# Taking the first 32 key tiles of the U table whole: turned and multiplied for all tokens on TensorE, gelu in pairs

## What is computed

```python
ia = jnp.take_along_axis(top_i[:, :, 0], best_c // K, axis=-1)
ib = jnp.take_along_axis(top_i[:, :, 1], best_c % K, axis=-1)
expert = ia * PEER_N_KEYS + ib
gate = jax.nn.softmax(best_s, axis=-1)
...
a = jnp.einsum('td,ted->te', xb, u_tab[eb])
hidden = gb.astype(xb.dtype) * jax.nn.gelu(a)
return jnp.einsum('te,ted->td', hidden, v_tab[eb])
```

## Time and profile before

| | us |
|---|---|
| median of three runs | 3085.14 |
| lowest, highest | 3076.94, 3086.59 |
| the profiled execution, its span | 3083.2 |
| first U row starts, last ends on VectorE | 1829.4, 2736.5 |
| busy in the span: TensorE, VectorE, ScalarE, POOL | 2723.6, 2111.9, 1146.2, 988.0 |

### The profile page before, as it was taken

One profiled execution on the slowest core, in us unless ns is written; L12 is line 12 of the kernel. 1 busy time (PEld: TensorE's weight loads), 2 busy tenths in 40 slices (PEclk: granted clock), 3 DMA queues, 4 the chain that ended last, 5 costly groups with the idle time before them and its releaser, 6 DMA issues.

```text
span 3083.2 us, 34652 instructions
## 1 busy us (share of the span) xinstructions
PE 2723.6 (88%) x12212; PEld 1969.0 (64%) x12212; DVE 2111.9 (68%) x2870; ACT 1146.2 (37%) x1980; POOL 988.0 (32%) x567
## 2 busy tenths in 40 slices
PE   9999999999999999999999975666666877669997
PEld 8888788888887888999889872222223433235433
DVE  5687665555564545445566688887888887679877
ACT  5455555555553335445665530000002330034000
POOL 0021000000000000000000038777778777878864
PEclk9999999999999999999999997898999888988999
DMA  7444455555555555453354459999999999999997
GB/s 271 151 155 164 173 178 183 189 190 190 190 177 191 184 185 183 178 182 135 127 191 173 164 228 415 419 409 410 408 417 411 416 407 402 420 376 383 409 402 305
DMA packets 123586, 827.89 MB, mean 269 GB/s; under 512 B 22167, under 2 KB 22183, under 8 KB 23855
## 3 DMA queue, kind: packets, MB, share of 16 engines
q0 software_dynamic: 79392, 510.36, 40.8%
q1 hardware_dynamic: 43920, 313.73, 28.5%
q10 hardware_dynamic: 144, 2.10, 0.2%
...
## 4 chain that ended last, share of the span: by engine, by line
PE 58%; POOL 14%; DMA 11%; DVE 9%; issue 5%; ACT 3%; DVEq 0%; SPq 0%; ACTq 0%
PE ps L608 49%; POOL rows L1324 14%; DMA rows<-peer_u,arena 7%; PE ps L1230 2%; DMA rows<-peer_v,arena 2%; DMA rows<-peer_v 2%; DVE arena L2449 2%; PE ps L1241 2%; DVE WL L506 1%; PE ps L716 1%; ACT arena L1800 1%; DVE arena L209 1%; DVE arena L202 1%; PE ps L916 0%; DVE arena L203 0%
## 5 line engine op out<-in xcount | busy, mean ns | idle before, releaser
L506 DVE SCALAR_TENSOR_TENSOR WL<-ring,PA,WH 128x512 fp32r<-128x512 f32 x896 | 633.1, 753 | 461.7 <-ACT WH L490 445.1
L1241 PE MATMUL ps<-rows,rstd 128*128 128x512 f32 x1164 | 629.6, 694 | 300.1 <-DMA rows<-peer_v,arena 216.9
L2449 DVE CUSTOM_DVE_ANT_0 arena<-rows,arena 128x2048 f32<-128x2048 f32 x256 | 586.9, 2293 | 155.7 <-DMA rows<-peer_u,arena 128.9
L1241 PEld LDWEIGHTS ps<-rows,rstd 128*128 128x128 f32 x1164 | 245.8, 221 | 670.5 <-issue 371.9
L1324 POOL DMA_INDIRECT rows<-peer_v,arena x256 | 484.0, 1891 | 196.8 <-DVE arena L2449 73.4
L489 ACT ACTIVATE WH<-ring,PA 128x512 fp32r<-128x512 f32 x448 | 324.2, 724 | 550.1 <-PE ps L608 401.7
L1324 POOL DMA_INDIRECT rows<-peer_u,arena x256 | 451.4, 1763 | 165.7 <-DVE WL L506 85.9
L608 PE MATMUL ps<-WH,HH 128*128 128x512 f32 x1120 | 442.8, 395 | 4.0 <-DVE WL L506 4.0
L608 PE MATMUL ps<-WH,HL 128*128 128x512 f32 x1120 | 438.0, 391 | 0.0
L608 PE MATMUL ps<-WL,HH 128*128 128x512 f32 x1120 | 437.9, 391 | 0.0
L490 ACT ACTIVATE WH<-ring,PA 128x512 fp32r<-128x512 f32 x448 | 317.2, 708 | 0.0
...
## 6 DMA issues: line engine op xcount, KB each, us to landing
ring<-stream SPq DMA_DIRECT2D x292, 1024.0 KB, 4.8
rows<-peer_v POOLq DMA_DIRECT2D x32, 1024.0 KB, 15.4
rows<-peer_u,arena POOLq DMA_INDIRECT x256, 14.8
rows<-peer_v,arena POOLq DMA_INDIRECT x256, 15.0
...
```

The source lines that it names most:

```text
L506: ins = nc.vector.scalar_tensor_tensor(out=half_tile(WL, u)[:, s], in0=raw_half(u)[:, s], scalar=gain[d], in1=half_tile(WH, u).bitcast(f32 ...
L1241: last = mm(ps[:, 4 * tt + q, :], DIAG[:, k % DIAGS, :], rows[:, SLOTS[n % ROWS], q * CH:(q + 1) * CH], start=n == mine[0], stop=n == ends[q])
L2449: ins = V.tensor_tensor_reduce(out=JUNK, in0=rows[:, SLOTS[n % ROWS], :], in1=HN[:, tt, :], scale=1.0, scalar=0.0, op0=ALU.mult, op1=ALU.a ...
```

## The change

- The 32 first tiles of U are loaded whole, too (`"turned"` entries, 2 per group in groups 0 to 7, 4 in groups 8 to 11, none later). TensorE transposes each, 16 blocks of 128 x 128 (`turn_u`, four parts of four), ScalarE copies each part to SBUF (`keep_turned_u`), and TensorE multiplies it with the transposed activations `HNT` for all 256 tokens (`u_products`, 16 products of 128 x 128 by 128 x 256). The parts 0 and 1 are transposed at the tile's entry; the rest (`finish_u`) comes after the next V row of TensorE, or before the next tile.
- Two tiles share a PSUM bank, and gelu is done for the pair, 128 x 512 elements: square and tanh on ScalarE (`square_u`, `tanh_u`), `poly_u` and `gelu_u` on VectorE, at fixed distances in `ROW_ORDER` (2, 5, 8 and 11 entries after the tile is finished).
- The batches now give gates instead of gate times gelu (`turn_ids` turns `GB`); VectorE multiplies them into the stored gelu (`weigh_dense`, two operations per batch), instead of ScalarE's copy. All 16 batches come in groups 12 to 15, one every 3.5 U rows.
- U gathers use the ids that leave the first 32 tiles out (one list, `IDU`; two copies fewer per `choose`).
- `choose` comes every 12 U rows from the 11th on, the last in group 9; `weigh` (three small operations) is split from `finish`.
- 9 V rows in groups 1 to 7 and 12 to 15, 5 in groups 8 to 11: 119 instead of 135 in the U stage (407 entries with the tiles) and 137 in the last. There one in eight V rows goes to TensorE (18 in all, 9 before), 119 to VectorE (112 before), and the V tiles start after V row 10 instead of 35.
- Before the first entry TensorE transposes `HN` (32 blocks) and ScalarE copies the result.

```diff
-LEAD = 9
 BATCH = 16
 BATCHES = P // BATCH
-DENSE_FROM, TAIL, SHARED = 35, 8, 3
-RING_OF = (16, 32)
+DENSE_FROM, TAIL, SHARED = 10, 8, 3
+LEADS = [0] + [9] * 7 + [5] * 4 + [9] * 4
+U_TILES = [2] * 8 + [4] * 4 + [0] * 4
+U_AFTER = {0: (), 2: (5, 12), 4: (1, 5, 9, 13)}
+PART_AT = (0, 6144, 12288, 10240)
+U_PARTS = (0, 2, 1, 3)
+U_ORDER = [8 * part + i for part in U_PARTS for i in range(8)]
 V_ORDER = [(g, j) for g in range(GROUPS) for j in range(PEER_K)]
-N_LEAD = LEAD * (GROUPS - 1)
...
     if m < 0:
         return True
-    if m < DENSE_FROM:
-        return m % 5 == 4
+    if m < N_LAST - TAIL:
+        return m % 8 == FIRST_V1 % 8
     return m in (N_LAST - TAIL + 1, N_LAST - TAIL + 3)
 ROW_ORDER = []
-_v = 0
+_v = _d = 0
 for _g in range(GROUPS):
     for _j in range(PEER_K):
         ROW_ORDER.append(("u", _g, _j))
-        if _g and LEAD * _j // PEER_K != LEAD * (_j + 1) // PEER_K:
+        if LEADS[_g] * _j // PEER_K != LEADS[_g] * (_j + 1) // PEER_K:
             ROW_ORDER.append(("v", *V_ORDER[_v]))
             _v += 1
-assert _v == N_LEAD
+        if _j in U_AFTER[U_TILES[_g]]:
+            ROW_ORDER.append(("turned", _d, 0))
+            _d += 1
+assert _v == N_LEAD and _d == N_DENSE
 ROW_LAST = len(ROW_ORDER)
 _d = 0
...
-_count = {"dve": 0, "pe": 0}
+RAW_TURNED = 24
+_count = {"dve": 0, "pe": 0, "turned": RAW_TURNED}
 for _tab, _g, _j in ROW_ORDER:
-    _by = "pe" if _tab == "dense" or _tab == "v" and by_matmul(PEER_K * _g + _j - N_LEAD) else "dve"
-    _count[_by] += 1
+    _by = "turned" if _tab == "turned" else "pe" if _tab == "dense" or _tab == "v" and by_matmul(PEER_K * _g + _j - N_LEAD) else "dve"
+    _count[_by] += 4 if _by == "turned" else 1
     ROW_DONE.append((_by, _count[_by]))
+FINISHED_AT = {}
+for _n, (_tab, _g, _j) in enumerate(ROW_ORDER):
+    if _tab == "turned":
+        FINISHED_AT[_g] = next(n for n in range(_n + 1, ROW_LAST) if ROW_ORDER[n][0] in ("v", "turned"))
+SQUARE_AT, POLY_AT, TANH_AT, GELU_AT = ({FINISHED_AT[2 * p + 1] + later: p for p in range(N_DENSE // 2)} for later in (2, 5, 8, 11))
 BATCH_AT = {}
-for _b in range(BATCHES):
-    BATCH_AT[ROW_AT["u", 9 + _b // 2, 3 + 8 * (_b % 2)]] = (0, _b)
-    BATCH_AT[ROW_AT["v", *V_ORDER[N_LEAD + 4 * _b + 3]]] = (1, _b)
-TURN_AT = {ROW_AT["u", 8, 3]: 0, ROW_LAST: 1}
+for _n in range(TT * BATCHES):
+    _g, _j = divmod(12 * PEER_K + 8 + 7 * _n // 2, PEER_K)
+    BATCH_AT[ROW_AT["u", _g, _j]] = divmod(_n, BATCHES)
+TURN_AT = {ROW_AT["u", 12, 4]: 0, ROW_AT["u", 14, 0]: 1}
 KEEP_AT = {n + 3: b for n, b in BATCH_AT.items()}
 ONE_HOT_AT = {n - 3: b for n, b in BATCH_AT.items()}
+U_ROWS = [(g, j) for g in range(GROUPS) for j in range(PEER_K)]
+CHOOSE_AT, GATE_AT, WEIGH_AT = ({ROW_AT["u", *U_ROWS[10 + 12 * (g - EARLY) + later]]: g for g in range(EARLY, GROUPS)} for later in (0, 3, 6))
+WEIGH_AT.update({ROW_AT["u", 0, 3 + 2 * g]: g for g in range(EARLY)})
 LAST_DENSE = ROW_AT["dense", N_DENSE - 1, 0]
 N_ROWS = len(ROW_ORDER)
...
+            def turn_u(n, d, part):
+
+                q = 4 * d + part
+                if part == 0:
+                    pe.wait_ge(sem(f"row_in{n % ROWS}"), 16 * (n // ROWS + 1))
+                if q >= 2:
+                    pe.wait_ge(sem("transposes_kept"), TT + q - 1)
+                else:
+                    pe.wait_ge(sem("norm_leading"), 8 * len(TURNED) + 8)
+                for k in range(4):
+                    at = (4 * part + k) * P
+                    last = nc.tensor.transpose(ps[:, 6 + q % 2, k * P:(k + 1) * P], rows[:, SLOTS[n % ROWS], at:at + P], ident)
+                last.then_inc(sem("raw_turned"), 1)
+
+            def u_products(d, part):
+
+                q = 4 * d + part
+                if d % 2 == 0 and part == 0 and d >= 4:
+                    pe.wait_ge(sem("gelu_done"), 1 + d // 2 - 1)
+                pe.wait_ge(sem("transposes_kept"), TT + q + 1)
+                for k in range(4):
+                    kt = 4 * part + k
+                    last = mm(ps[:, 4 + d // 2 % 2, d % 2 * TOK:(d % 2 + 1) * TOK], UT[q % 2][:, k, :], HNT[kt // 8][:, kt % 8, :],
+                              start=kt == 0, stop=kt == KD - 1)
+                last.then_inc(used, 1)
+
+            def finish_u(n, d):
+
+                u_products(d, 0)
+                turn_u(n, d, 2)
+                u_products(d, 1)
+                turn_u(n, d, 3)
+                u_products(d, 2)
...
-                    pool.wait_ge(sem(f"rows_{by}"), count)
-                if tab == "dense":
-                    pool.dma_start(rows[:, SLOTS[n % ROWS], :], v_tab[g * PEER_KEYS:(g + 1) * PEER_KEYS, :]).then_inc(sem(f"row_in{n % ROWS}"), 16)
+                    pool.wait_ge(sem({"dve": "rows_dve", "pe": "rows_pe", "turned": "raw_turned"}[by]), count)
+                if tab in ("dense", "turned"):
+                    table, ia = (v_tab, g) if tab == "dense" else (u_tab, U_ORDER[g])
+                    pool.dma_start(rows[:, SLOTS[n % ROWS], :], table[ia * PEER_KEYS:(ia + 1) * PEER_KEYS, :]).then_inc(sem(f"row_in{n % ROWS}"), 16)
                     continue
...
+            def keep_turned_u(d, part):
+
+                q = 4 * d + part
+                act.wait_ge(sem("raw_turned"), RAW_TURNED + q + 1)
+                if q >= 2:
+                    act.wait_ge(used, 2 * N_TILES + q - 1)
+                A(UT[q % 2], ps[:, 6 + q % 2, :].rearrange("p (k i) -> p k i", i=P), ACT.Copy).then_inc(sem("transposes_kept"), 1)
+
...
+            def square_u(p):
+
+                act.wait_ge(used, 2 * N_TILES + 8 * p + 8)
+                if U_ORDER[2 * p] // 8 in (2, 3):
+                    act.wait_ge(sem("gate_arg"), PEER_H * (U_ORDER[2 * p] // 8 - 1))
+                if U_ORDER[2 * p] // 8 == 1:
+                    act.wait_ge(sem("rows_dve"), ROW_DONE[ROW_AT["u", PEER_H - 1, PEER_K - 1]][1])
+                A(dense_hidden(p), ps[:, 4 + p % 2, :], ACT.Square, scale=math.sqrt(0.044715)).then_inc(sem("squares"), 1)
+
+            def tanh_u(p):
+
+                act.wait_ge(sem("gelu_poly"), 1 + p + 1)
+                v = dense_hidden(p)
+                A(v, v, ACT.Tanh, scale=math.sqrt(2 / math.pi)).then_inc(sem("gelu_tanh"), 1)
...
-                ch.link(V.tensor_tensor(SKIP, SKIP, ID, ALU.add))
-                ch.link(V.tensor_copy(IDV[:, tt * PEER_E + 16 * h:tt * PEER_E + 16 * h + 16], SKIP))
-                ch.mark(V.tensor_copy(IDU[:, tt * PEER_E + 16 * h:tt * PEER_E + 16 * h + 16], ID), "experts_ready")
+                ch.mark(V.tensor_tensor(IDU[:, tt * PEER_E + 16 * h:tt * PEER_E + 16 * h + 16], SKIP, ID, ALU.add), "experts_ready")
...
+            def weigh(g):
+
+                tt, h = g // PEER_H, g % PEER_H
+                es = slice(16 * h, 16 * h + 16)
+                dve.wait_ge(sem("gate_exp"), g + 1)
+                ch.link(V.reciprocal(RC, SM8[:, tt, h:h + 1]))
+                ch.link(V.tensor_scalar(GB[:, tt, es], GA[:, tt, es], RC, 0.5, ALU.mult, ALU.mult))
+                ch.mark(V.scalar_tensor_tensor(out=GM[:, tt, es], in0=IAF[:, tt, es], scalar=float(N_DENSE), in1=GB[:, tt, es],
+                                               op0=ALU.is_ge, op1=ALU.mult), "gates_ready")
+
...
-                ch.link(V.tensor_scalar(RC, SM8[:, tt, h:h + 1], 2.0, None, ALU.mult))
-                ch.link(V.reciprocal(RC, RC))
+                es = slice(16 * h, 16 * h + 16)
                 dve.wait_ge(sem("peer_tanh"), g + 1)
                 ch.link(V.scalar_tensor_tensor(out=x, in0=PO, scalar=1.0, in1=x, op0=ALU.add, op1=ALU.mult))
-                gathered = GA[:, tt, 16 * h:16 * h + 16]
-                ch.link(V.scalar_tensor_tensor(out=x, in0=x, scalar=RC, in1=gathered, op0=ALU.mult, op1=ALU.mult))
-                ch.mark(V.scalar_tensor_tensor(out=gathered, in0=IAF[:, tt, 16 * h:16 * h + 16], scalar=float(N_DENSE), in1=x,
-                                               op0=ALU.is_ge, op1=ALU.mult), "hidden")
+                ch.mark(V.tensor_tensor(GA[:, tt, es], x, GM[:, tt, es], ALU.mult), "hidden")
...
+            def poly_u(p):
+
+                dve.wait_ge(sem("squares"), 8 + 8 * len(TURNED) + p + 1)
+                v = arena[:, DENSE_AT[U_ORDER[2 * p]]:DENSE_AT[U_ORDER[2 * p]] + 2 * TOK]
+                V.scalar_tensor_tensor(out=v, in0=v, scalar=1.0, in1=ps[:, 4 + p % 2, :], op0=ALU.add, op1=ALU.mult).then_inc(sem("gelu_poly"), 1)
+
+            def gelu_u(p):
+
+                dve.wait_ge(sem("gelu_tanh"), 1 + p + 1)
+                v = arena[:, DENSE_AT[U_ORDER[2 * p]]:DENSE_AT[U_ORDER[2 * p]] + 2 * TOK]
+                V.scalar_tensor_tensor(out=v, in0=v, scalar=1.0, in1=ps[:, 4 + p % 2, :], op0=ALU.add, op1=ALU.mult).then_inc(sem("gelu_done"), 1)
+
+            def weigh_dense(tt, b):
+
+                n = BATCHES * tt + b
+                dve.wait_ge(sem("dense_h"), n + 1)
+                if n == 0:
+                    dve.wait_ge(sem("gelu_done"), 1 + N_DENSE // 2)
+                t = slice(tt * P + b * BATCH, tt * P + (b + 1) * BATCH)
```

(14 more changed lines are left out.)

145 lines of the change are left out of this document (95 added, 50 removed).

## The result

| | before | after |
|---|---|---|
| median (lowest to highest), us | 3084.44 (3076.94 to 3086.59) | 3149.62 (3147.76 to 3160.35) |
| span of the profiled execution | 3083.2 | 3146.0 |
| first U row starts | 1829.4 | 1822.8 |
| U stage | 907.1 | 948.4 |
| last stage | 346.7 | 374.8 |

The ratio is 1.0221, 95% interval 1.0206 to 1.0237: slower by 65 us, where 25 us less was forecast.

The account below looks back on a forecast made before the run. Transfers were taken to bound the U stage, VectorE and TensorE after the change. U stage -37 us and last stage +12 took the span from 3083.2 to 3058; the median, 2 us over, was 3060, range 3025 to 3102.

Parts of the forecast that it names:

- the bytes: Whole kernel: left-out U rows cost no bandwidth, so the page's bytes must fall by 33 to 34 MB.
- VectorE's own time: U stage: VectorE's work with small gaps goes from 778 us to 824, over the transfers' 794.
- TensorE's work: U stage: V rows, tiles at 9.5 us each and gate batches sum to 785 us at full clock.
- case A: U stage: VectorE and TensorE take over from the transfers; about a third of 83 us arrives, 3038 to 3080; chance 52%.
- I allow 7 us: 870: U stage: the largest engine times by section add to 863; 7 us for imperfect interlocking gives 870, -37 us.
- the cover of the `HN` transposes: Ahead of the U stage: 32 transposes and 8 copies, some 9 us, fall in TensorE's idle time and cost nothing.
- the last stage, +12: Last stage: +31 us of bytes from 16 moved V gathers, less credits for dips, net +12 (+5 to +20).
- dips: Last stage: moving eight batches away saves 10.6 us from 2745 to 2815 and about 8 us of lesser dips.
- D: Groups 1 to 11: TensorE is the bound, with lower clock and ScalarE's order holding V rows; slower, 3106; chance 19%.
- C: U stage: POOL's issue of gathers is the bound, so no change; 3077 to 3095; chance 15%.
- the lock: U stage: beside VectorE's rows POOL issues one gather per row, 2.44 us; 119 others need 154 us outside rows.

Follow-up runs that it names:

- experiment 1: Changed kernel with each tile's second half transposed, copied and multiplied at the tile's own entry, not behind the next V row: 3106.83 us, 1.0071 to the kernel before.
- experiment 6: Kernel of experiment 1 with the 64 whole-tile loads issued from SyncE's queue instead of POOL's: 3099.9 us, 1.0063 to the kernel before.
- experiment 10: Changed kernel, second half at once, tile loads on SyncE, first three exponentials earlier, `weigh_dense` and gelu steps from `poly_u` on later: 3096.21 us, 1.0041.
- Experiment 5: Kernel of experiment 4 with VectorE's second U-product operand read from a PSUM bank in groups 1 to 7: 2999.35 us, 0.9729 to the kernel before.
- experiment 4: Kernel before with one edit: U gathers leave out the first 32 tiles, no U tile loaded instead: 3024.65 us, 0.9806 to the kernel before.
- experiment 8: Kernel of experiment 1 with the last stage's plan of V rows and tiles as in the kernel before: 3108.18 us, 1.0078.
- experiment 9: Changed kernel with the second half at once and three of four U products of each tile left out: 3096.28 us, 1.0043 to the kernel before.
- experiment 3: Changed kernel with three of four products of every U tile part left out, the second half still put off: 3115.62 us, 1.0109.

## Why the prediction was wrong

**Right: the bytes.** 33 to 34 MB less were foreseen, 34.2 measured in all (827.89 to 793.69). That the transfers stopped setting the stage was right as well.

**Right: VectorE's own time.** 824 us foreseen. After: 948.4 less its waits (62.6, 25.8, 12.8 at line 2626, 10.3 at line 2602, 7.7) is 829. The tiles' strided steps, the least certain price, were cheap. Groups of VectorE in the U stage:

```profile
L2609 DVE SCALAR_TENSOR_TENSOR arena<-arena,ps 128x512 f32<-128x512 f32 x16 | 11.0, 688 | 62.6 <-ACT arena L1908 62.6
...
L2626 DVE TENSOR_TENSOR arena<-arena,ps 128x384 f32<-128x384 f32 x16 | 8.8, 552 | 13.5 <-PE ps L1291 12.8
...
L2628 DVE TENSOR_TENSOR arena<-arena,ps 128x128 f32<-128x128 f32 x16 | 4.5, 280 | 0.0
```

A gelu step is 0.69 us (0.70 foreseen), a `weigh_dense` 0.83 plus gaps (1.0).

**Right: TensorE's work.** Of TensorE's groups in the stage, lines 1260 and 1249 sum to 121.1 + 121.0 + 72.5 = 315 us, 9.8 a tile against 9.5, and the engine was busy 797 us against 785.

**A slip in the range of case A.** A U stage of 893 and a last stage of +20 make 3091, not 3080. The measured time lies beyond both.

**Wrong: the step from the sums to the stage, "I allow 7 us: 870".** The largest engine time in each section was taken as the section's length, and everything that one engine makes another wait for was put into 7 us. In fact it was 78 us more. The runs split it so: 47 us the second half put off behind the V row (experiment 1), which made VectorE wait 62.6 us for squares and POOL 128.4 us for slots, and cost the time mostly through the squares; then, by profiled executions and within their scatter, 10 us the tiles' issue on POOL (experiment 6, 891.4), and 1.6 more with the cover of group 0 (next point) and the later steps (experiment 10, 889.8; the cover alone gave 3.3). That leaves 20 us over 870 which none of the mends took, and their cause stays open. There VectorE waits 49 us for rows while POOL waits 100 us for slots. Experiment 5 makes the issue of gathers beside VectorE's rows the likely one, since in the kernel of experiment 4 it was a bound; in the changed kernel the PSUM operand was not tried.

**Wrong: the cover of the `HN` transposes, "nothing, and 9 us if that cover were gone".** The first U row was not delayed, so TensorE's side was covered. ScalarE's 8 copies were not: the exponentials of groups 0 to 2 stood behind them in its program, and VectorE's `weigh(0)` waited 7.7 us. The copies took 4.0 of these (1831.97 to 1836.00 on ScalarE); the rest is that `weigh(0)` now stands after the fourth U row, where before the first use of an exponential was in `finish`, at the end of the group. The question asked was "is TensorE idle then?"; it should have been "what stands behind the copies on ScalarE, and who needs it now?". Group 0 took 59.8 us; 52 was foreseen, and 52.1 it is with the order mended.

**Wrong: the last stage, +12.** The bytes were right: 346.7 us at 370 GB/s are 128.3 MB, 374.8 at 376 are 140.9, 12.6 more, and 31 us at 409 GB/s. The 18.6 us credited for dips were not. Windows of the kernel before, the dip:

```profile
2736.50:2761.50 25.00, 14.15 (x48) 9.90 (x47) 21.70 (x25) 17.04 (x46) 14.20 (x10) 0.70 0.99 396
2761.50:2786.50 25.00, 23.62 (x126) 16.61 (x125) 23.73 (x15) 20.15 (x50) 18.44 (x10) 0.89 0.76 273
2786.50:2811.50 25.00, 23.33 (x110) 16.54 (x110) 23.51 (x15) 22.44 (x57) 21.65 (x13) 0.80 0.96 357
```

and the rest of the stage, in the kernel before and in the kernel after:

```profile
2811.50:3036.50 225.00, 215.94 (x516) 95.75 (x515) 181.92 (x78) 2.16 (x6) 165.46 (x110) 0.98 1.00 408
```

```profile
2796.20:3121.20 325.00, 285.40 (x625) 121.44 (x624) 249.62 (x107) 6.02 (x15) 227.59 (x151) 0.96 0.99 395
```

The dip lost 75 x (1 - 342/409) = 12 us, where 18.6 had been credited, and it did go. But from 2796 to 3121 the kernel after averages 395 GB/s, where the kernel before had 408 from 2811 to 3036: 3% of 325 us, 10 us, came back spread thin. With the 31 us of bytes that makes +29, against the 28.1 measured. What holds the rate at 395 stays open; experiment 8 rules out only the plan of V rows and tiles.

**The rivals.** D had the mechanism by name: its signs were that POOL waits for the transposes' line and VectorE at the gelu steps for squares, and both came (its third, a clock under 0.93, did not: 0.94). But it tied them to TensorE's total, "once TensorE needs more than 43 us per 12 U rows". Experiments 1 and 9 show that the position behind the V row matters 47 us, and the total 10 once that is mended; with the second half put off the total matters 34 to 40 (experiment 3). That D's 3106 meets the kernel of experiment 1, from which the delay is gone, is chance. The delay could have been seen in the order ahead of the run: between a tile's entry and its last products stood a V row, and in group 0 that V row can't start before the group ends. C's mechanism, the lock, was there too and limits the gain (experiments 4 and 5), beneath the delay. A was refuted: neither VectorE (774 of 948) nor TensorE (797) set the stage. The range, 3025 to 3102, ended below D's own figure, and the mechanism cost more than D said.
